# Shorter bias lookup, packed constants, column tiles, and output runs laid through a recurrence, in one decoder layer

## The reference, cut to what is computed

```python
x = swiglu_half(x, ...)            # x + 0.5 * FFN(rms_norm(x))
x = x + mixer(rms_norm(x))
x = swiglu_half(x, ...)

def compress(rows, w1, b1, w2, b2):   # 32-token blocks, stride 16
    ...
        h = h + jnp.einsum('bngf,fe->bnge', ch[:, r:r + n_cmp], w1[r])
    return jnp.einsum('bnge,ed->bngd', jax.nn.silu(h), w2) + b2
```

## Time and profile before

| | |
|---|---|
| median of 3 runs | 2903.29 us (2899.12 to 2904.34) |
| the profiled execution's own time | 2907.07 us |
| its span in the trace | 2905.3 us |
| mean granted clock of TensorE | 0.981 |
| TensorE busy | 2863.4 us, 99% of the span, 19432 matmuls |
| VectorE, ScalarE, GpSimd busy | 1475.8, 1005.9, 96.9 us |
| chain that ended last | PE 94%, DVE 3%, ACT 2%, issue 1% |

### The profile page before, as it was taken

One profiled execution on the slowest core, in us unless ns is written; L12 is line 12 of the kernel. 1 busy time (PEld: TensorE's weight loads), 2 busy tenths in 40 slices (PEclk: granted clock), 3 DMA queues, 4 the chain that ended last, 5 costly groups with the idle time before them and its releaser, 6 DMA issues.

```text
span 2905.3 us, 47966 instructions
## 1 busy us (share of the span) xinstructions
PE 2863.4 (99%) x19432; PEld 2730.3 (94%) x19432; DVE 1475.8 (51%) x1852; ACT 1005.9 (35%) x1150; POOL 96.9 (3%) x169
## 2 busy tenths in 40 slices
PE   8999999999999999999999989999999999999999
PEld 5789999999999999998888879899999999999999
DVE  4434444434444444446667777585444434444433
ACT  3433334223223233333332253344333223223222
POOL 2110000000000011100000000010000000000000
PEclk9999999999999999998999998789999999999999
DMA  8364455455455454533336761436555455455454
GB/s 217 100 205 131 145 153 154 138 150 170 145 150 153 127 163 149 209 133 116 119 110 212 230 204 54 123 117 188 146 154 147 130 149 171 145 152 151 128 149 136
DMA packets 637326, 437.54 MB, mean 151 GB/s; under 512 B 20109, under 2 KB 621901, under 8 KB 629661
## 3 DMA queue, kind: packets, MB, share of 16 engines
q1 hardware_dynamic: 634210, 419.13, 47.9%
q0 software_dynamic: 2608, 13.71, 1.5%
q10 hardware_dynamic: 380, 2.93, 0.3%
HBM read 422.33 MB, written 21.65 MB: 153 GB/s over the span
## 4 chain that ended last, share of the span: by engine, by line
PE 94%; DVE 3%; ACT 2%; issue 1%; SPq 1%; DMA 0%; ACTq 0%; POOLq 0%; POOL 0%; DVEq 0%
PE bank L419 64%; PE bank L766 11%; PE bank L1769 4%; PE bank L690 2%; PE bank L692 2%; PE bank L691 2%; ACT whi L745 1%; PE bank L2225 1%; PE bank L1928 1%; PE bank L1390 1%; PE bank L1180 1%; PE bank L485 0%; PE bank L1938 0%; DVE wlo L750 0%; PE bank L1336 0%
## 5 line engine op out<-in xcount | busy, mean ns | idle before, releaser
L324 DVE TENSOR_TENSOR wlo<-wraw,whi 128x2048 fp32r<-128x2048 f32 (+1 forms) x305 | 612.6, 2008 | 509.2 <-ACT whi L320 485.8
L320 ACT ACTIVATE whi<-wraw 128x2048 fp32r<-128x2048 f32 (+1 forms) x305 | 513.1, 1682 | 679.5 <-PE bank L419 679.5
L419 PE MATMUL bank<-xl,whi 128*128 128x320 f32 x2816 | 441.8, 309 | 0.0
L419 PE MATMUL bank<-xh,whi 128*128 128x320 f32 x2816 | 441.8, 309 | 0.0
L419 PE MATMUL bank<-xh,wlo 128*128 128x320 f32 x2816 | 441.6, 309 | 0.0
L419 PEld LDWEIGHTS bank<-xl,whi 128*128 128x128 f32 x2816 | 420.2, 188 | 0.2
L419 PEld LDWEIGHTS bank<-xh,whi 128*128 128x128 f32 x2816 | 420.1, 188 | 0.1
L419 PEld LDWEIGHTS bank<-xh,wlo 128*128 128x128 f32 x2816 | 420.2, 188 | 0.0
L419 PE MATMUL bank<-hl,whi 128*128 128x320 f32 x1408 | 227.3, 309 | 0.0
L419 PE MATMUL bank<-hh,whi 128*128 128x320 f32 x1408 | 227.3, 309 | 0.0
L419 PE MATMUL bank<-hh,wlo 128*128 128x320 f32 x1408 | 227.3, 309 | 0.0
(11 more groups left out here) (338 smaller groups left out, 2810.0 us busy)
## 6 DMA issues: line engine op xcount, KB each, us to landing
wraw<-in_w_ffn_gate_up SPq DMA_DIRECT2D x176, 1024.0 KB, 5.4
wraw<-in_w_ffn_down SPq DMA_DIRECT2D x128, 704.0 KB, 4.5
wraw<-in_w_mix SPq DMA_DIRECT2D x52, 1024.0 KB, 5.0
pages<-in_cache_cmp SPq DMA_DIRECT2D x128, 128.0 KB, 2.0
oraw<-in_w_mix_out SPq DMA_DIRECT2D x32, 512.0 KB, 3.5
k_sel<-in_slc_k SPq DMA_DIRECT2D x64, 128.0 KB, 2.5
s_v<-in_slc_v SPq DMA_DIRECT2D x64, 128.0 KB
o_win_sample<-in_state_win_kv POOLq DMA_DIRECT2D x8, 1008.0 KB, 15.0
```

The costliest lines, as they stand in the source:

```text
L320: act.activation(whi[:, a % 2, 0:size], wraw[:, a % RAW, 0:size], ACT.Copy).then_inc(s["hi_ready"], 1)
L324: dve.tensor_tensor(wlo[:, a % 2, 0:size], wraw[:, a % RAW, 0:size], whi[:, a % 2, 0:size].bitcast(F32), ALU.subtract).then_inc(s["lo_read ...
L419: mm = pe.matmul(b, w[:, a % 2, c], x[:, kk, :], start=first, stop=end)
```

## The change

The parts, in the order of the program:

1. The one-hot matrix keeps only the 1168 columns of all distances (3 blocks instead of 13), and the table is loaded ahead of it.
2. The first unit's 16 pages are issued by three queues, SP 6, ACT 5 and POOL 5. The first-layer weights come as a quarter and three quarters; ACT issues the second part behind its pages.
3. Twenty loads of constants become six packed ones, issued behind POOL's pages.
4. The second layer for sample values, and the prompt's first layer, run as two column halves of 64 that write different partitions of the same bank; the prompt's first layer has twice as many matmuls.
5. The sample's running values (L1390) run on four column quarters of 32, 208 instructions instead of 104.
6. cpb is no longer loaded but copied by DVE out of tb, after a fill with a large negative value. bb comes from 16 loads instead of 48, with DVE copies that reverse or stride, and the window's mask is added.
7. In the recurrence, an output tile is issued in three runs of 8 matmuls. RUNS says how many runs stand within a beat (between two halves of the scores, or of a head) and how many at its end; OUT_AT follows from it (tile 0 at beat 0, then 1, 2, 3, 5, 6, 7, 8, 10, 11, 13, 14, 16, 17, 18, 19). Results first run the eight products of the carried state, then the eight of the masked scores, these over all 128 rows, with am in two buffers that are cleared once, and 64 rows of vt cleared by POOL.

```diff
-NB_ROWS = -(-C_ALL // 512)
+NB_ROWS = -(-LF // 512)
...
-                    mm = pe.matmul(bank[7][:, 64 * et:64 * et + 64], w1p[:, v, r, j, et * P:(et + 1) * P],
-                                   chp_[v][:, j, r:r + 64], start=(r, j) == (0, 0), stop=(r, j) == (1, 7))
+                    for e in (0, 64):
+                        mm = pe.matmul(bank[7][e:e + 64, 64 * et:64 * et + 64], w1p[:, v, r, j, et * P + e:et * P + e + 64],
+                                       chp_[v][:, j, r:r + 64], start=(r, j) == (0, 0), stop=(r, j) == (1, 7))
...
-                    for b in range(nb):
-                        o = (g * nb + b) * HD
-                        for et in range(2):
+                    for et in range(2):
+                        for b in range(nb):
...
+        SP_PAGES, ACT_PAGES, POOL_PAGES = 6, 5, 5
...
-                    for i in range(2):
-                        sp.dma_start(cpb[:, i, :, :], bias_ap(C_CP + i * P * 16, [[16, P], [C_ALL, HEADS], [1, 16]])
-                                     ).then_inc(s["cpb_ld"], 16)
...
+                for j, x in enumerate((96, 224)):
+                    link(dve.tensor_copy(cpb[:, j, 4 * g:4 * g + 4, 0:x // 16 + 1], tb_[:, g % 2, :, x::-16]))
...
-                        for par in range(2):
-                            r, d0, q0 = slice(64 * par, 64 * par + 64), g2 * P + 64 * par, 64 * g2 + 32 * par
-                            lhs = s_v[:, kt, d0:d0 + 64] if kt < 12 else vnb[:, d0:d0 + 64]
+                        for r0 in range(0, P, 32):
+                            r, d0, q0 = slice(r0, r0 + 32), g2 * P + r0, 64 * g2 + 32 * (r0 // 64)
+                            lhs = s_v[:, kt, d0:d0 + 32] if kt < 12 else vnb[:, d0:d0 + 32]
...
-                link(dve.tensor_copy(bb[:, 0:1032], bbr[:, 1031::-1]))
-                link(dve.tensor_copy(bb[:, 1032:1552], bbr[:, 1551:1031:-1]))
-                link(dve.tensor_copy(bb[:, 1552:1616], bbr[:, 1552:1616]))
+                link(dve.tensor_copy(bb[:, 0:NSB], bbr[:, NSB - 1::-1]))
+                link(dve.tensor_copy(bb[:, 1032:1552], bbr[:, 519::-1]))
+                link(dve.tensor_tensor(bb[:, 1032:1032 + TS], bb[:, 1032:1032 + TS], wmask[:, :], ALU.add))
+                link(dve.tensor_copy(bb[:, 1552:1615], bbr[:, 1000::-16]))
+                link(dve.memset(bb[:, 1615:1616], NEG))
...
+        RUNS = [(1, 1), (1, 2)] * 4 + [(1, 2), (0, 1)] + [(1, 1)] * 8 + [(0, 4), (0, 4)]
+        FIRST_RUN = [sum(sum(r) for r in RUNS[:b]) for b in range(BEATS + 1)]
+        OUT_AT = {b: -(-FIRST_RUN[b] // 3) for b in range(BEATS) if -(-FIRST_RUN[b] // 3) * 3 < FIRST_RUN[b + 1]}
...
+            if c:
+                for h in range(HG):
+                    pe.matmul(o(h), st[:, h, :], qi_[:, c % 2, h, :], start=h == 0, stop=False, skip_group_check=True)
             for h in range(HG):
-                o = bank[5][:, h * 64:(h + 1) * 64]
-                mm = pe.matmul(o, vt[r, i, h * P:(h + 1) * P], am[r, h, :], start=True, stop=c == 0)
-                if c:
-                    mm = pe.matmul(o, st[:, h, :], qi_[:, c % 2, h, :], start=False, stop=True)
+                mm = pe.matmul(o(h), vt[:, i, h * P:(h + 1) * P], am_[c % 2][:, h, :], start=c == 0 and h == 0,
+                               stop=h == HG - 1, skip_group_check=True)
...
+                if h < 0:
                     if b % 2 == 0:
-                        pe_hgrn_scores(pe, b // 2)
-                    elif b // 2 < NC:
-                        pe_hgrn_results(pe, b // 2)
-                elif b - 10 < HG:
-                    pe_head(pe, b - 10)
-                if b >= 12:
-                    pe_head_sum(pe, b - 12)
-                if b in OUT_AT:
-                    pe_out(pe, OUT_AT[b])
+                        pe_hgrn_scores(pe, c, range(0, 2) if c < NC else range(1))
+                    pe_out_runs(pe, b, 0)
+                    if b % 2 == 0:
+                        if c < NC:
+                            pe_hgrn_scores(pe, c, range(2, 4))
+                        pe_hgrn_keys(pe, c)
+                    elif c < NC:
+                        pe_hgrn_results(pe, c)
+                elif h < HG:
+                    pe_head(pe, h, 0)
+                    pe_out_runs(pe, b, 0)
+                    pe_head(pe, h, 1)
+                    pe_head_state(pe, h)
+                if h >= 2:
+                    pe_head_sum(pe, h - 2)
+                pe_out_runs(pe, b, 1)
...
             act.dma_start(onehot[:, :], io["c_onehot"]).then_inc(s["ld_table"], 16)
-            act.dma_start(table[0:32, :], io["rel_bias_table"]).then_inc(s["ld_table"], 16)
-            for half in range(2):
-                act.dma_start(*first_layer(0, half)).then_inc(s[f"w1_ld{half}"], 16)
+            act.dma_start(*first_layer(0, 0)).then_inc(s["w1_ld0"], 16)
+            act.wait_ge(s["ld_pt"], 16)
+            for k in range(SP_PAGES, SP_PAGES + ACT_PAGES):
+                load_page(act, 0, k)
+            act.dma_start(*first_layer(0, 1)).then_inc(s["w1_ld1"], 16)
...
+            for k in range(SP_PAGES + ACT_PAGES, 16):
+                load_page(pool, 0, k, "rows_ldp")
```

More of the change, by code:

```diff
@@ L173, in build @@
         w2 = at("w2", 204.75, [P, 2, 2, HD])
-        onehot = at("onehot", 8.125, [33, C_ALL])
+        onehot = at("onehot", 8.125, [33, LF])
         q2 = at("q2", 4.125, [P, 2, 4, T])
@@ L586, in sync_cached @@
                 if u == 2:
-                    for half in range(2):
+                    for part in range(2):
                         sp.wait_ge(s["w1_lo"], 8)
-                        sp.dma_start(*first_layer(1, half)).then_inc(s[f"w1_ld{half}"], 16)
+                        sp.dma_start(*first_layer(1, part)).then_inc(s[f"w1_ld{part}"], 16)
         def act_first_layer(act, v, j):
-            act.wait_ge(s[f"w1_ld{j // 4}"], 16 * v + 16)
+            act.wait_ge(s[f"w1_ld{min(j // 2, 1)}"], 16 * v + 16)
             if v:
@@ L1308, in dve_att @@
                 if (n, step) == (0, 0):
-                    dve.wait_ge(s["cpb_ld"], 32)
+                    link(dve.memset(cpb[:, :, :, :], NEG))
                     dve.wait_ge(s["g_p"], 1)
@@ L1755, in dve_out_evict, with pe_out_run, pe_out_runs, pe_hgrn_scores @@
             dve.tensor_tensor(xt[:, m, :], xt[:, m, :], bank[i % 2][:, 0:T], ALU.add).then_inc(s["o_ev"], 1)
[L1757 to L1774 removed]
+        def pe_out_run(pe, i, run):
+            w, xs = ((ohi, xh), (ohi, xl), (olo, xh))[run]
+            if run == 0:
+                pe.wait_ge(s["o_hi"], i + 1)
+                if i >= 2:
+                    pe.wait_ge(s["o_ev"], i - 1)
+            if run == 2:
+                pe.wait_ge(s["o_lo"], i + 1)
+            for k in range(8):
+                x = 8 * (i // KT) + k
+                if i % KT == 0 and run < 2:
+                    pe.wait_ge(s["x_hi" if run == 0 else "x_lo"], x + 1)
+                c = slice(k * P, (k + 1) * P)
+                mm = pe.matmul(bank[i % 2][:, 0:T], w[:, i % 2, c], xs[:, x, :], start=run == 0 and k == 0,
+                               stop=run == 2 and k == 7)
+            if run == 2:
+                mm.then_inc(s["o_done"], 1)
+        def pe_out_runs(pe, b, part):
+            first = FIRST_RUN[b] + sum(RUNS[b][:part])
+            for r in range(first, first + RUNS[b][part]):
+                pe_out_run(pe, r // 3, r % 3)
+        def pe_hgrn_scores(pe, c, ks):
             a = bank[2]
[L1776 removed]
+            if c and ks[0] == 0:
                 pe.wait_ge(s["h_am"], 4 * c)
[L1778 removed]
+            for k in ks:
                 pe.wait_ge(s["h_mul2"], 4 * c + k + 1)
@@ L2064, in mix_dve @@
             dve_in(dve, link)
-            link(dve.memset(am[:, :, :], 0.0))
+            for k in range(2):
+                link(dve.memset(am_[k][:, :, :], 0.0))
             dve_out(dve, 0)
@@ L2326 @@
     arrays, io = {}, {}
-    named = [(n, np.ascontiguousarray(inputs[n])) for n in _INS] + list(_constants().items()) + _layouts(inputs)
+    consts = _constants()
+    named = ([(n, np.ascontiguousarray(inputs[n])) for n in _INS] + [(n, a) for n, a in consts.items() if n not in ("c_pair", "c_same")]
+             + _layouts(inputs, consts))
     for name, a in named:
```

217 lines of the change are left out of this document (102 added, 115 removed).

## The result

The changed kernel takes 2878.26 us (2874.10 to 2880.14, 4 runs), the kernel before 2903.65 on the same chip: a ratio of 0.9914, with a 95% interval from 0.9897 to 0.9931. It is faster, by 25 us instead of the 57 that were forecast, and lies 10 us above the range. The profiled execution's own time is 2878.76 us (span 2877.1, mean clock 0.986). Two executions far off all others, 5939.64 us of the kernel before and 4211.72 us of the first kernel under "All of it together", were slow and are left out of every figure here.

What follows compares the result with a forecast made beforehand. TensorE, busy 99% of the span, was taken to bound the kernel. Terms −15 − 4 − 6.6 + 1 − 6 − 27 = −57.6 gave 2849.5 us profiled, 2846 at the median; range 2829 to 2868.

Steps and rivals of the forecast that it cites:

- Running values: Line 1390, eight groups: quarters take 1.6 us instead of 3.15, but SP's queue limits the gain to −6 us.
- Rival 2: Line 1390: column quarters do not run beside each other, +25 us instead of −6; total −26.6, 2877 us; chance 0.08.
- The start: Before the first compression product: issue binds the pages; product starts at 15 to 16 us instead of 31.36, −15 us.
- the moved load: At the start: ACT issues the second part of the weights behind its five pages, at about 10 us, at no cost.
- Rival 3: The start is bound by transfers at 209 GB/s: first product at 25 us, total −48.6, 2855 us; chance 0.10.
- Second layer and prompt first layer: Lines 505 and 485, on two column halves: 2.01 to 1.0 us and 3.52 to 1.87 us per group, −4 and −6.6.
- Bias: Loads of cpb and bb: fewer loads on SP, more small VectorE operations, +1 us (0 to +3).
- Recurrence: Stage from 1755 to 1916 us: grouped results, split and moved outputs, less low clock; 133.4 of 161 us, −27.
- the wait at the results of chunk 2: Recurrence, beat 3: ScalarE's split waits for output 2, so TensorE newly waits about 3 us before these results.
- Rival 5: Recurrence: more hand-overs make the clock fall and stay low, stage +74 us, total +43, 2947 us; chance 0.06.
- The floor of about 25 ns: Line 1390: matmul starts never closer than this, 5.2 us an iteration, +16.4 in all instead of −6; 2868 us.

Runs made afterwards that it cites:

- the first kernel under "All of it together": The changed kernel with running values in two bursts (last sequence halves), odd beats reordered, second unit's pages held back, five unread lookup products: 2848.52 us, ratio 0.9821.

## Why the prediction was wrong, step by step

- **Running values: the step that failed.** The term was −6 and measured +12.13. It took 1.6 us a group, held back by SP's queue. The price of the products was about right (1.96 us). The queue was not: from the first to the second group, with no stop between, the period is 22.58 us, near the 22.5 that were given as its floor, but in the runs with another order of beats and with the weights moved it is 22.14, all of the 1.26 us by which a group became shorter, with no idle time of TensorE in it. TensorE's own work sets the period, and the products would have given −10. What is missing is a term: 104 matmul records more per sequence are as many more instructions, weight loads with them, and they are used up at three times the pace (9.4 ns a record instead of 31). Waiting for the next block of them cost 15.61 us, and the low clock behind the stops up to 6.8 more. The text put the supply of instructions at nothing; it stood in no row that I read, since at the old pace it never ended last. Rival 2 gave nearly this total (−26.6 against −28.2), but by another mechanism, and the runs exclude it: that its total fits is chance.
- **The start.** The pages were said to be bound by their issue, with the first product at 15 to 16. Issue was over at 9, and the pages were late all the same, because three quarters of the weights, which the text had moved "at no cost" behind ACT's five pages, stood in the transfers ahead of the last pages of SP and POOL. With the weights behind all the pages the first product starts at 14.96. The trace of the kernel before had a row for this that the text did not read: the forecast counted two microseconds from issue to landing, but the 16 pages of the first unit took

```profile
DMA to landing us min/median/max: 4.5/11.0/13.9
```

The first of them, issued at 3.00, landed at 13.62, behind weights issued at 1.79 and 2.25 that landed at 11.85 and 17.26. So the step was right on the pages and wrong on the moved load: it was priced on its own queue, and not at the engines that all queues share. Here the Trainium skill, "DMA: Bandwidth & Descriptors", section "Issuing engines are not separate DMA queues", was closer than I allowed: the engines are shared, whoever issues. The trace agrees: SP's last page took 9.52 us to land behind ACT's weights and 4.65 without them ahead of it. Rival 3's 25 us, from a mean rate of 209 GB/s, was too slow; the engines carried 320 to 390 between 8 and 18 us.
- **Second layer and prompt first layer.** Sized a little high: 2.01 to 1.08 and 3.52 to 2.02 us. In the second layer four groups of 0.93 us should be 3.7, and 2.1 arrived between the first compression product and the FFN. The last group is the reason for most of it: it waits 2.21 us for VectorE where it waited 1.51 us for ScalarE, and the clock is low from 215.60 to 219.01, so that it takes 1.62 us instead of 1.08. The +1.05 of the FFN behind it is the same low clock; in the run with another order of beats, where the clock did not fall here, the two stretches took 195.78 and 930.17 us.
- **Bias.** +1 forecast, +1.44 measured up to the first running value, which is less than the spread of that stretch between traces; no run tests this part by itself.
- **Recurrence.** The best step: −27 forecast, −26.8 in the changed kernel and −26.7 with this part alone, of which 2.3 and 2.4 come back behind the middle of the outputs. The mechanism was right: between the first scores and the middle of the outputs the low clock lasts 33.0 us instead of 84.2, which at half speed is 25.6 us, and the results of a chunk take 3.69 us where the clock is full, as forecast (3.7); TensorE's idle time grew from 0.9 to 5.5 us there. Within it the wait at the results of chunk 2 was found at its place and sized right as a wait (3 forecast, 3.58 measured), but its price was 10 us, since the clock stays low after it. The split of the term was off, and that the total fits so closely is partly luck: from the first scores to the first head's products it went from 98.6 to 82.8 us, −16 where −24 was forecast (the 10 us of chunk 2 are in it), and from there to the last unbroken row of outputs from 77.3 to 67.7, −9.6 where −3.4 was forecast. Part of this is a slip in the sum: the text moves 10.6 us of output work into the head part, but the first ten beats had 30 runs and RUNS leaves them 24, so six runs of 1.17 us move, 7.0. In the head part VectorE carries the chain now, as the text had it, but the hand-overs cost less than a microsecond a head: VectorE is busy 60.74 of the 67.69 us.
- **Chances.** Rival 5, the slower side, asked for a clock that falls at every hand-over; it rose. The range left out a cost that no row bounded, and the bounds of the running values (−11.6, and +25 in rival 2) did hold the +12.1; the range cut that off, because the weight was put on the lower half.

## What to carry to other kernels

When a change makes instructions smaller and more, ask how fast the engine uses them up, not only how long each lasts: a burst that outruns the loading of instructions stops for microseconds, and spreading it between long instructions (163.25 us for the running values here) or keeping fewer, larger ones (165.24) beat the shorter matmuls in one burst (178.19). A transfer that moves to another queue still stands ahead of everything issued after it on the shared engines, so order loads by when they are needed, over all queues. Where a wait lets TensorE's clock fall, price it with the low clock that follows: here 3.6 us of waiting cost 10.

## What the runs showed of the hardware

- **Instructions have a pace.** In the changed kernel, groups of 208 matmul records at 9.4 ns broke off after 143 to 193 of them for 1.9 to 4.4 us, and resumed 1.24 to 1.47 us after a 16384-byte block had landed; 208 records at 30 ns never did. The Trainium skill, "Runtime: NRT & Kernel Launch", section "Instruction fetch mechanics", has instructions come in 16 KiB blocks of 256, with the cost of a boundary mostly hidden. The trace agrees on the block, since the stops lie multiples of 256 instructions apart; with 416 records in a group (weight loads included) one burst spans more than a block, and the cost is not hidden at this pace.
- **Four column tiles run beside each other.** 208 records in 1.96 us are 9.4 ns from start to start. The floor of about 25 ns that the prediction quoted from the Trainium skill, "TensorE: Matmul & The Clock Gate", section "Wait — 56ns, not 53.3ns?", does not bind matmuls that lie in different column quarters.
- **The first products run at the low clock either way.** They start 0.43 us apart at first, and the clock rises 4.65 us after the first of them where TensorE idled 11.66 us before (changed kernel), 3.24 us after it where TensorE was busy with lookup products until the last moment (0.17 us of idle time), and 3.22 to 5.54 us after it in the other runs with such idle time.
- **A page waits behind another queue's transfer.** A page issued by SP at 8.70 us, behind the second part of the weights that ACT had issued at 7.99, took 9.52 us to land; with those weights issued after the pages it took 4.65 (with only the second unit's pages held back, 9.85).
